# Low-rank columns cut as 128 and 64, low-rank products in turn by row group, and one joined score tile per head in the HGRN output (one Trainium2 core)

## The reference, cut to what matters

```python
p = h @ w_in                      # 5*512 HGRN columns, then RWKV columns
# RWKV columns: r, k, v (512 each), lwf, lwb, la (32 each), lg (96)
w_logit = dir_stack(w0[0] + jnp.tanh(lwf) @ w_decay2[0], w0[1] + jnp.tanh(lwb) @ w_decay2[1])
a = jax.nn.sigmoid(a0 + la @ w_a2)
g = jax.nn.sigmoid(lg) @ w_g2
# HGRN, per head and direction, chunks of tokens, bc = cumsum(log f):
o_inter = jnp.einsum('nbhcd,nbhde->nbhce', qq * jnp.exp(bc), s)
scores = jnp.einsum('nbhtd,nbhsd,nbhtsd->nbhts', qq, kk, decay)     # decay is 0 where s is after t
o = o_inter + jnp.einsum('nbhts,nbhse->nbhte', scores, vv)
s_new = jnp.exp(blast[..., 0, :])[..., None] * s + jnp.einsum('nbhsd,nbhse->nbhde', kk * jnp.exp(blast - bc), vv)
```

## Time and profile before

| what | us |
|---|---|
| median of 3 runs | 4412.87 |
| lowest, highest | 4408.31, 4414.9 |
| the profiled execution | 4408.46 |
| its span in the trace | 4406.5 |
| TensorE busy in the span | 4009.7 (91%) |
| VectorE busy | 2103.1 (48%) |
| ScalarE busy | 1153.5 (26%) |
| GpSimd busy | 1200.8 (27%) |

### The profile page before, as it was taken

One profiled execution on the slowest core, in us unless ns is written; L12 is line 12 of the kernel. 1 busy time (PEld: TensorE's weight loads), 2 busy tenths in 40 slices (PEclk: granted clock), 3 DMA queues, 4 the chain that ended last, 5 costly groups with the idle time before them and its releaser, 6 DMA issues. The chain is left out here.

```text
span 4406.5 us, 104834 instructions
## 1 busy us (share of the span) xinstructions
PE 4009.7 (91%) x40636; PEld 2703.8 (61%) x40636; DVE 2103.1 (48%) x3820; ACT 1153.5 (26%) x2839; POOL 1200.8 (27%) x1508
## 2 busy tenths in 40 slices
PE   7999699999987999999999867877999999999987
PEld 5888567676757888888898734444333343343333
DVE  2221277677755666666666468883111111111116
ACT  1111144444433444443444322320000000000001
POOL 0000011111111554554545344424222222222220
PEclk8999799999998999999999988886999999999999
DMA  9711366555544333334433264424658999999987
GB/s 364 183 70 51 97 214 195 199 193 196 195 164 147 126 121 116 127 106 130 131 94 127 75 201 134 141 79 174 239 219 306 396 392 402 392 407 420 420 341 314
DMA packets 322551, 925.08 MB, mean 210 GB/s; under 512 B 67272, under 2 KB 164776, under 8 KB 273440
## 3 DMA queue, kind: packets, MB, share of 16 engines
q1 hardware_dynamic: 268368, 772.01, 48.8%
q0 software_dynamic: 46928, 131.38, 8.2%
q10 hardware_dynamic: 6912, 16.78, 1.0%
HBM read 969.46 MB, written 208.53 MB: 267 GB/s over the span
## 5 line engine op out<-in xcount | busy, mean ns | idle before, releaser
L2723 PE MATMUL exp_gate_up<-exp_w_gate,exp_rows_and_rowsT 128*64 128x512 f32 x1664 | 731.3, 596 | 14.9 <-DMA exp_w_up<-in_moe_w_up_dram 13.7
L2723 PE MATMUL exp_gate_up<-exp_w_up,exp_rows_and_rowsT 128*64 128x512 f32 x1664 | 731.8, 596 | 0.0
L2723 PEld LDWEIGHTS exp_gate_up<-exp_w_gate,exp_rows_and_rowsT 128*64 128x64 f32 x1664 | 227.5, 138 | 483.7 <-issue 483.7
L869 PE MATMUL rwp_product<-rwp_hT,rwp_w_rw 128*128 128x256 f32 (+1 forms) x1936 | 420.8, 380 | 10.0 <-DVEq L804 10.0
L2674 DVE TENSOR_TENSOR exp_hidden<-exp_hidden,exp_gate_up 64x512 f32<-64x512 f32 x104 | 72.0, 692 | 702.4 <-ACT exp_hidden L2655 702.4
L869 PEld LDWEIGHTS rwp_product<-rwp_hT,rwp_w_rw 128*128 128x128 f32 (+1 forms) x1936 | 361.0, 187 | 67.6 <-issue 10.4
L1047 PE MATMUL hgp_product<-hgp_hT,const_w_hg 128*128 128x256 f32 x1664 | 379.3, 383 | 8.7 <-DVEq L1028 8.7
L2748 PE MATMUL exp_down<-exp_w_down,exp_hiddenT 128*64 128x512 f32 x1664 | 380.0, 597 | 3.3 <-DMA exp_w_down<-in_moe_w_down_dram 0.4
L1047 PEld LDWEIGHTS hgp_product<-hgp_hT,const_w_hg 128*128 128x128 f32 x1664 | 313.9, 192 | 60.6 <-issue 11.0
L2655 ACT ACTIVATE exp_hidden<-exp_gate_up 64x512 f32<-64x512 f32 x104 | 61.3, 589 | 953.8 <-PE exp_gate_up L2723 953.8
L2632 POOL DMA_INDIRECT s_yb<-exp_out,exp_row_slot x104 | 104.3, 1003 | 567.6 <-PE exp_rows_turned L2708 442.0
(11 more groups left out here) (424 smaller groups left out, 7123.7 us busy)
## 6 DMA issues: line engine op xcount, KB each, us to landing
exp_w_gate<-in_moe_w_gate_dram SPq DMA_DIRECT2D x208, 1024.0 KB
exp_w_up<-in_moe_w_up_dram SPq DMA_DIRECT2D x208, 1024.0 KB
exp_w_down<-in_moe_w_down_dram SPq DMA_DIRECT2D x104, 2048.0 KB
s_rw_in<-prep_operands SPq DMA_DIRECT2D x72, 514.0 KB, 3.9
rw_operands<-s_rw_in SPq DMA_DIRECT2D x72, 514.0 KB, 7.9
hg_qkf<-s_hg_in SPq DMA_DIRECT2D x36, 768.0 KB, 9.7
rw_tokens<-s_rw_tm SPq DMA_DIRECT2D x144, 192.0 KB, 4.9
const_w_hg<-in_w_mod_dram SPq DMA_DIRECT2D x24, 1024.0 KB, 17.0
```

The source lines that it names most:

```text
L869: mm = nc.tensor.matmul(mp[o % 2][0:width, 0:GROUP], w_in[:, k, c0 - 5 * D_HG:c0 - 5 * D_HG + width], hT[b][:, k, :], start=(k == 0), stop ...
L2723: i = nc.tensor.matmul(pgu[u][q:q + BLK], xT[:, k, r * BLK:(r + 1) * BLK], w[r][:, k, :], start=(k == 0), stop=(k == KD - 1))
```

## The change

Three edits, each with its bookkeeping.

1. The 192 low-rank columns are cut as 128 and 64 instead of 96 and 96. Output 12 now holds the three low-rank inputs and the first 32 gate columns, output 13 the other 64 gate columns. Output 13 is computed in two halves of 128 tokens, which go to the two halves of the PSUM partitions; ScalarE copies it out in two pieces. The prep takes the sigmoid of the gate in two pieces, and the gate weights are loaded in the same changed order.
2. The low-rank products of a prep run over kinds inside, head pairs outside. All three banks must be empty before the first product, and all three are released at the end.
3. In the HGRN output the two diagonal 64x64 blocks and the crossing block stand in one 128x128 tile `all[d]` per head (the fourth block stays zero). VectorE's merge of tasks 14 and 15 writes its block there, ScalarE copies the two diagonal blocks in (a new step at `HG_JOIN`, semaphore `joined`), and TensorE computes one product per head where it had three.

```diff
...
 NPAIR = 4
 LORA = 32
 GATE_LORA = 96
+GATE_HEAD = P - 3 * LORA
+GATE_REST = GATE_LORA - GATE_HEAD
 D_IN = 5 * D_HG + 3 * D_RW + 3 * LORA + GATE_LORA
 HG_STEPS = (CTX + LAT) // 128
 RW_C = 64
...
 HG_TASKS = 16
-HG_LOG, HG_SUM, HG_ENDS, HG_OUT = 0.0, 0.02, 0.045, 0.90
+HG_LOG, HG_SUM, HG_ENDS, HG_JOIN, HG_OUT = 0.0, 0.02, 0.045, 0.78, 0.90
 
 
 def hg_time(t):
...
         self.diff = [sb(f"exponent{r}", [P, HH, P]) for r in range(4)]
         self.z = [sb(f"scaled_qk{r}", [P, HH, P]) for r in range(4)]
         self.sc = [sb(f"scores{d}", [P, HH, RW_C]) for d in range(2)]
-        self.sc6 = [sb(f"scores_across{d}", [P, HH, RW_C]) for d in range(2)]
+        self.all = [sb(f"scores_all{d}", [P, HH, P]) for d in range(2)]
         self.eb = [sb(f"decay_from_start{d}", [P, HH, P]) for d in range(2)]
         self.ekb = [sb(f"decay_to_end{d}", [P, HH, P]) for d in range(2)]
         self.khT = [sb(f"k_tokens{d}", [P, HH, P]) for d in range(2)]
...
                 act.wait_ge(s["k_turned"], 2 * n + dd + 1)
                 nc.scalar.activation(self.khT[dd][:], self.pst[:], ACT.Copy).then_inc(s["k_copied"], 1)
         for d in range(2 if full else 0):
+            yield HG_JOIN + 0.05 * d
+            act.wait_ge(s["combined"], 16 * m + 12 + d + 1)
+            wait(act, s["out_done"], 2 * (m - 1) + d + 1)
+            for a in range(2):
+                i = nc.scalar.activation(self.all[d][HALF[a], :, HALF[a]], self.sc[d][HALF[a]], ACT.Copy)
+            i.then_inc(s["joined"], 1)
+        for d in range(2 if full else 0):
             yield HG_OUT + 0.05 * d + 0.02
             act.wait_ge(s["out_done"], 2 * m + d + 1)
             wait(act, s[f"stored{d}"], 16 * m)
...
             if full:
                 pe.wait_ge(s["q_scaled"], 2 * m + d + 1)
                 pe.wait_ge(s["combined"], 16 * m + 14 + d + 1)
+                pe.wait_ge(s["joined"], 2 * m + d + 1)
                 if d == 0 and isinstance(n, int) and n == HG_CTX:
                     pe.wait_ge(s["state_zero"], 4)
                 wait(pe, s["state_updated"], 2 * (n - 1) + d + 1)
...
                 pe.sem_inc(s["turns"], 1)
                 v = [self.v[u][d][:, h * P:(h + 1) * P] for h in range(HH)]
                 for h in range(HH):
-                    for a in range(2):
-                        nc.tensor.matmul(self.po[HALF[a], h, :], self.sc[d][HALF[a], h, :], v[h][HALF[a]], start=(h == 0), stop=False,
-                                         skip_group_check=True)
-                for h in range(HH):
-                    nc.tensor.matmul(self.po[HALF[1 - d], h, :], self.sc6[d][:, h, :], v[h], start=False, stop=False, skip_group_check=True)
+                    nc.tensor.matmul(self.po[:, h, :], self.all[d][:, h, :], v[h], start=(h == 0), stop=False, skip_group_check=True)
                 for h in range(HH):
                     mm = nc.tensor.matmul(self.po[:, h, :], self.eb[d][:, h, :], self.st[d][:, h, :], start=False, stop=(h == HH - 1),
                                           skip_group_check=True)
...
             dve.wait_ge(s["scored"], 16 * m + t + 1)
             wait(dve, s["combined"], 16 * m + t - 1)
             if t < 2:
-                wait(dve, s["out_done"], 2 * (m - 1) + d + 1)
+                wait(dve, s["joined"], 2 * (m - 1) + d + 1)
                 nc.vector.tensor_tensor(self.sc[d][:], self.psc[t % 2][:], K["idc"][:].unsqueeze(1).broadcast_to([P, HH, RW_C]),
                                         ALU.mult).then_inc(s["combined"], 1)
             elif t < 14:
...
                                           self.psc[t % 2][:]).then_inc(s["combined"], 1)
             else:
                 wait(dve, s["out_done"], 2 * (m - 1) + d + 1)
-                nc.vector.tensor_copy(self.sc6[d][HALF[d]], self.psc[t % 2][HALF[d]]).then_inc(s["combined"], 1)
+                nc.vector.tensor_copy(self.all[d][HALF[d], :, HALF[1 - d]], self.psc[t % 2][HALF[d]]).then_inc(s["combined"], 1)
 
         for d in range(2):
             yield HG_SUM + 0.01 * d
...
         w_loaded = [m.sem(f"w_loaded{b}") for b in range(len(blocks))]
         mod = Modulation(nc, m, S, A, K, K["w_hg"])
 
-        outs = [(5 * D_HG + j * P, P) for j in range(12)] + [(5 * D_HG + 12 * P, GATE_LORA), (5 * D_HG + 12 * P + GATE_LORA, GATE_LORA)]
+        outs = [(5 * D_HG + j * P, P) for j in range(13)] + [(5 * D_HG + 13 * P, GATE_REST)]
         NO = len(outs)
         dead = lambda g, o: isinstance(g, int) and g == 0 and (o < 4 or o == NO - 1)
 
...
                     pool.wait_ge(s["act_freed"], 7 * g + 7)
                     pool.wait_ge(s["dve_freed"], 7 * g + 7)
                     ctx_group = isinstance(g, int) and g == 0
-                    for lo, hi, rows in ((4, 12, P), (12, 13, GATE_LORA)) if ctx_group else ((0, 12, P), (12, 14, GATE_LORA)):
+                    for lo, hi, rows in ((4, 12, P), (12, 13, P)) if ctx_group else ((0, 13, P), (13, 14, GATE_REST)):
                         dst = S["rw_ctx"] if ctx_group else S["rw_lat"]
                         off = 1 if ctx_group else g * GROUP - GROUP + GRID_W
                         pool.dma_start(dst[lo:hi, 0:rows, bass.ds(off, GROUP)].rearrange("t p c -> p t c"),
...
                         if dead(g, o):
                             act.sem_inc(s["act_freed"], 1)
                             continue
-                        width = outs[o][1]
-                        nc.scalar.activation(ro[b][0:width, o, :], mp[1][0:width, 0:GROUP], ACT.Copy).then_inc(s["act_freed"], 1)
+                        if o == NO - 1:
+                            for u in range(2):
+                                i = nc.scalar.activation(ro[b][0:GATE_REST, o, u * P:(u + 1) * P], mp[1][HALF[u], 0:P], ACT.Copy)
+                        else:
+                            i = nc.scalar.activation(ro[b][:, o, :], mp[1][:, 0:GROUP], ACT.Copy)
+                        i.then_inc(s["act_freed"], 1)
 
                 mod.act_start(act)
                 mod.act_copy(act)
...
                         if dead(g, o):
                             dve.sem_inc(s["dve_freed"], 1)
                         else:
-                            width = outs[o][1]
-                            nc.vector.tensor_copy(ro[b][0:width, o, :], mp[0][0:width, 0:GROUP]).then_inc(s["dve_freed"], 1)
+                            nc.vector.tensor_copy(ro[b][:, o, :], mp[0][:, 0:GROUP]).then_inc(s["dve_freed"], 1)
                         if ahead and o == 6:
                             norm_stats(g + 2, b)
                         if ahead and o == 8:
...
                             pe.wait_ge(w_loaded[0 if c0 < blocks[0][1] else 1], 16 * KD)
                         freed, each = (s["dve_freed"], s["act_freed"])[o % 2], 7
                         wait(pe, freed, each * g + o // 2)
+                        c = slice(c0 - 5 * D_HG, c0 - 5 * D_HG + width)
                         for k in range(KD):
-                            mm = nc.tensor.matmul(mp[o % 2][0:width, 0:GROUP], w_in[:, k, c0 - 5 * D_HG:c0 - 5 * D_HG + width], hT[b][:, k, :],
-                                                  start=(k == 0), stop=(k == KD - 1))
+                            if o < NO - 1:
+                                mm = nc.tensor.matmul(mp[o % 2][:, 0:GROUP], w_in[:, k, c], hT[b][:, k, :], start=(k == 0), stop=(k == KD - 1))
+                                continue
+                            for u in range(2):
+                                mm = nc.tensor.matmul(mp[o % 2][HALF[u], 0:P], w_in[:, k, c], hT[b][:, k, u * P:(u + 1) * P],
+                                                      start=(k == 0), stop=(k == KD - 1))
                         mm.then_inc(s["product_done"], 2 if dead(g, o + 1) else 1)
 
                 pe.wait_ge(mod.s["ident_ready"], 1)
...
 
     def consts(self, sp):
         A, s = self.A, self.s
-        sp.dma_start(self.mu[:, 0:12], A["rw_mu"][0, 0:12 * P].rearrange("(t p) -> p t", p=P)).then_inc(s["consts"], 16)
-        sp.dma_start(self.mu[0:GATE_LORA, 12:14], A["rw_mu"][0, 12 * P:].rearrange("(t p) -> p t", p=GATE_LORA)).then_inc(s["consts"], 16)
+        sp.dma_start(self.mu[:, 0:13], A["rw_mu"][0, 0:13 * P].rearrange("(t p) -> p t", p=P)).then_inc(s["consts"], 16)
+        sp.dma_start(self.mu[0:GATE_REST, 13:14], A["rw_mu"][0, 13 * P:].rearrange("(t p) -> p t", p=GATE_REST)).then_inc(s["consts"], 16)
         for j, src in enumerate((A["rw_w0"][0, 0], A["rw_w0"][0, 1], A["rw_a0"][0], A["rw_k_k"][0], A["rw_k_a"][0],
                                  A["rw_r_k"][0].rearrange("h j -> (h j)"))):
             sp.dma_start(self.col[:, j, :], src.rearrange("(t p) -> p t", p=P)).then_inc(s["consts"], 16)
         for d in range(2):
             sp.dma_start(self.w2[d * LORA:(d + 1) * LORA, :], A["rw_w_decay2"][0, d]).then_inc(s["consts"], 16)
         sp.dma_start(self.w2[2 * LORA:, :], A["rw_w_a2"][0]).then_inc(s["consts"], 16)
-        sp.dma_start(self.g2[:], A["rw_w_g2"][0]).then_inc(s["consts"], 16)
-
-    N_CONSTS = 16 * 12
```

(21 more changed lines are left out.)

5 lines of the change are left out of this document (2 added, 3 removed).

## The result

The changed kernel takes **4347.8 us** (median of 4 runs, 4341.6 to 4352.7) against 4410.9 for the kernel before beside it (4 runs, 4408.3 to 4414.9): a ratio of 0.9855, 95% interval 0.9838 to 0.9872, 63 us faster. The forecast was 4357 us and faster. The profiled execution was the slowest of the four, 4352.65 us (span 4351.1), 55.4 less in the span than the one of before. In two later sets on other chips the same kernel was 68.6 and 65.7 us faster than the kernel before by the medians, so the 55 us of this pair of traces is at the low end of what the change brings.

A forecast was written before the change was run, and what follows sets the result against it. The prediction took TensorE to bound the projection, second stage and scans, with waits on ScalarE and VectorE in the second stage. It summed 11.3 + 13 + 31 = 55 us off 4408.5, and 4.4 for the median: 4357 us, range 4336 to 4385.

The forecast's parts named there:

- Last output, 11.3 us: First projection stage: paired column halves cut the last output from 3.49 to 2.08 us, 1.41 saved in each of 8 groups.
- Low-rank order, 13 us: Second stage, 18 blocks: three row groups overlap, 1.1 us saved per block; 8.8 in first preps, 5 in second, less 9 x 0.1.
- I count five late ones of 1 us, 5: Second preps: in five of 9, TensorE reaches the transposes late, so the block's saving counts, 1 us each.
- The 0.9 us for the later release: Low-rank blocks of the 9 second preps: the first result is released about 0.1 us later, as all three go together.
- HGRN join, 31 us: Scans: two output sets become one of 0.99 us per direction; 1.93 us saved per step, in 16 steps.
- The 0.1 credited for L560: Scans, direction 1: the shape change of about 0.1 us inside L560's 1.06 moves ahead of that direction's output set.
- A: Clock rival: half-rate pieces shift in scans and second stage; ten more give 4369 us, ten fewer 4345; chance 0.13.
- B: Low-rank block: three row groups don't overlap, block takes 2.6 us and first release comes 1.5 later; 4387 us, chance 0.05.
- F: Whole change: joined set costs what the two did and neither packing overlaps; about 4415 to 4408 us, chance 0.03.
- C: Projection's last output: column halves don't pair, 3.83 us instead of 3.49, so 11.3 becomes -2.7; 4371 us, chance 0.05.
- E: Scans: direction 1's join holds up the second X copy and TensorE; 4423 us at 4.1 lost per step; chance 0.04.
- D: All 18 low-rank blocks pay in full, 20 us instead of 13, and shape changes are cheaper; 4348 us, chance 0.08.

The follow-up runs named there:

- split_alone: The kernel before with only the low-rank columns cut as 128 and 64 and what hangs on their places: 4396.5 us against 4407.9, ratio 0.9972.
- halves_in_turn: The changed kernel with the last projection output's two halves computed one after the other: 4348.8 us, 15.3 slower than the changed kernel in its set.
- join_slow: The changed kernel with four extra ScalarE copies of 64x256, read by nothing, ahead of each join: 4362.2 us, 25.3 slower than the changed kernel.

## Why the prediction was right, and where its terms were off

**The bound.** Right in the projection, in the first preps and in the scans: work taken from TensorE came out of the span. In second preps at full clock it didn't; the waits behind the block grew instead, as the prediction had said. They went from 5.8 to 11.4 us at the transposes, with 4 to 6 more forecast.

**Last output, 11.3 us.** Right: a full group is 1.41 us shorter, the very number, and 11.0 us came in the end. The pairing was argued from 64 and 512 columns, and 128 lies between them. Two small errors cancel in the 1.41. The 16 products of before are 3.45 us from start to start and not 3.49. After, the 1.90 of the output, 0.09 more idle time ahead of it and 0.06 more in the transposes behind it make 2.05, where 2.08 was forecast.

**Low-rank order, 13 us.** The block takes 1.10 us, as forecast. With the order alone, the first preps of the eight groups after the first gain 7.8 us, not 8.8: most gained 1.01, as the wait for tanh grew from 1.26 to 1.35. The very first prep's block runs at half clock and gains 2.0 instead of nothing. The step that failed is "I count five late ones of 1 us, 5". The five were there, and their intervals are 9.8 us shorter together with the order alone (10.0 for all eight). The prediction named no reason for their lateness. The traces show one: half-clock stretches that began in the block itself. I had read the earlier trace rows, a late arrival at 753.76, and not asked what had made it late: from 736.8 us on, in the block before it, the clock was at half for 6.8 us. The 0.9 us for the later release isn't there: the sigmoids begin 1.16 us after the block's start in both kernels. The sum, 19.9, is 7 above the term; in the changed kernel, with its own half-clock stretch near the first block, the stretch gains 16.0 to 17.4.

**HGRN join, 31 us.** Right in mechanism and 0.26 us a step too small: the output section saves 2.28 us and a shape change ahead of it costs 0.09. The sum had four prices wrong. The 0.99 us of L554, taken as the price of one set, has a change of shape in it: the product with the state is 0.89 behind a set of its own shape, and that is 0.10 saved in each direction which the sum lacks. The 0.1 credited for L560 isn't there (1788.67 to 1789.72 is 1.05 still). The change ahead of direction 0 costs 0.09 and not 0.17, and the two sets of direction 1 give 1.07 and not 1.00. In steps at full clock TensorE is busy 60.9 to 61.6 us, where it was 63.2 to 63.5 in all but the last; such steps last 64.1 to 66.2 us, around the 65.2 forecast. Two such steps of the changed kernel (TensorE, the second execution):

```profile
1584.00:1648.10 64.10, 61.06 (x1579) 1.00 0.41 126
...
2306.10:2371.20 65.10, 61.09 (x1579) 1.00 0.39 123
```

The intervals gained 2.13, 2.37 and 2.52 us in the three executions and 2.43 with the join alone. What lies beside 2.19 isn't explained. There are fewer half-clock stretches in the 15 intervals (7 to 9, 10 before), but split_alone has only 6 and its intervals are no shorter, 1017.1 us. The copies cost 0.83 us a join instead of 0.76, and the slack was 0.32 instead of 0.4.

**Rivals.** A went the other way: the clock gave a good part of the order's gain. In the stretch of the low-rank blocks the half-clock time went from 34 us in 6 stretches to 20 in 3 (10 in 2 with the order alone). B and F fell by the traces of the changed kernel. (B's own price was a little high: its first release comes after 20 of 24 instructions and not 22, so 1.3 us late and not 1.5.) C fell by the 1.90 us of the output, and halves_in_turn shows why; E fell by the slack that join_slow measured. D's 4348 is the time that came, but by luck: it asked for all 18 blocks to pay in full, and at full clock the second preps paid nothing.

**The total.** 55 us forecast, 63 to 69 measured by the medians. The range held it; the likeliest value was 9 us too high. Most of what is missing lies in two terms that were too small, the low-rank order and the HGRN set.

## What to carry to other kernels

A late arrival in a trace wants its cause before it is priced: compare the same stretch at both granted clocks, and see where each half-clock piece begins. If pieces begin in one sparse block behind a wait, try a denser order for it: here that brought them from 21 in 36 blocks to 7 in 81. A row's length can hold a change of shape; price a set from a row whose neighbours have the shape it will have. Where an engine's wait follows a block, its gain counts only up to that wait; the next step is the chain that ends it, and there the order of results matters more than their sum.
